# A bidirectional scan kernel: the stores of the raw diagonal blocks change their place and, in part, their queue

## What is computed

```
def step(S, inp):
    r_t, w_t, k_t, v_t, kk_t, kka_t = inp
    sa = einsum('bdhvk,bdhk->bdhv', S, kk_t)
    S = (S * w_t[..., None, :] - sa[..., :, None] * kka_t[..., None, :]
         + v_t[..., :, None] * k_t[..., None, :])
    return S, einsum('bdhvk,bdhk->bdhv', S, r_t)
```

## Time and profile before

| | us |
|---|---|
| three timed executions | 4001.73, 4027.17, 4028.21 (median 4027.17) |
| profiled execution, its own time | 3987.78 |
| its span in the trace | 3986.0 |
| TensorE busy | 3632.5 (91 %) |
| GpSimd busy | 1079.8 (27 %) |
| VectorE busy | 1378.7 (35 %) |
| ScalarE busy | 783.3 (20 %) |

### The profile page before, as it was taken

How to read it: one execution, slowest core, us unless ns; L and a number is a source line. 1 busy time by engine, 2 the same in 40 slices (tenths; PEclk the granted TensorE clock), 3 DMA queues, 4 the chain that set the end, 5 groups by cost and what they waited for, 6 DMA issues and landing times. The chain is left out here.

```text
span 3986.0 us, 64120 instructions
## 1 busy us (share of the span) xinstructions
PE 3632.5 (91%) x24967; PEld 2877.3 (72%) x24968; DVE 1378.7 (35%) x2811; ACT 783.3 (20%) x1467; POOL 1079.8 (27%) x1573
## 2 busy tenths in 40 slices
PE   8999999995799999999799999999999949999960
PEld 4777666663699889999788989989989934444420
DVE  2444444442345454454122222222222242222237
ACT  1222222222233333232111111111111101111113
POOL 0333333333555555555011011011011000000013
PEclk9999999997899999999899999999999969999985
DMA  8323222223323333332711011111011144765235
GB/s 290 106 100 105 97 95 91 91 96 136 88 74 97 102 101 101 95 91 52 244 69 64 35 41 64 35 41 64 35 41 64 41 166 164 258 230 185 89 111 206
DMA packets 297255, 424.33 MB, mean 106 GB/s; under 512 B 122446, under 2 KB 206156, under 8 KB 297036
## 3 DMA queue, kind: packets, MB, share of 16 engines
q1 hardware_dynamic: 268812, 309.84, 23.8%
q10 hardware_dynamic: 16272, 67.64, 4.5%
q0 software_dynamic: 11952, 43.52, 3.3%
HBM read 287.99 MB, written 132.94 MB: 106 GB/s over the span
## 5 line engine op out<-in xcount | busy, mean ns | idle before, releaser
L1757 PE MATMUL c_ps<-c_hT,big 128*128 128x128 f32 x6528 | 751.3, 276 | 27.3 <-DMA big<-in_w_in 27.3
L1757 PEld LDWEIGHTS c_ps<-c_hT,big 128*128 128x128 f32 x6528 | 742.6, 193 | 35.3 <-issue 30.1
L661 PE MATMUL a_ps<-a_win,a_hT 128*128 128x512 f32 (+1 forms) x1088 | 416.1, 540 | 3.8 <-DVE a_mix L572 3.8
L2180 PE MATMUL e_ps<-big,e_xT 128*128 x784 | 347.6, 597 | 2.3 <-DVE e_xT L2142 2.3
L661 PEld LDWEIGHTS a_ps<-a_win,a_hT 128*128 128x128 f32 x1088 | 204.0, 190 | 199.8 <-issue 187.0
L655 PE MATMUL a_ps<-a_hT,a_win 128*128 128x128 f32 x2992 | 343.9, 277 | 2.3 <-ACT a_hT L343 2.3
L655 PEld LDWEIGHTS a_ps<-a_hT,a_win 128*128 128x128 f32 x2992 | 340.6, 193 | 6.2 <-issue 2.9
L1110 POOL TENSOR_TENSOR b_tmp<-b_tt,b_ta 128x126 f32<-128x126 f32 (+22 forms) x527 | 203.7, 386 | 332.4 <-DMA b_ta<-s_a 269.5
L2180 PEld LDWEIGHTS e_ps<-big,e_xT 128*128 128x128 f32 x784 | 149.4, 191 | 191.8 <-issue 191.8
L1757 PE MATMUL c_ps<-c_wo,c_mT 128*128 128x512 f32 x544 | 236.3, 592 | 0.0
L1722 DVE TENSOR_TENSOR c_gs<-c_gs,c_ps 128x384 f32<-128x384 f32 x136 | 75.3, 554 | 445.1 <-PE c_ps L1757 434.9
(11 more groups left out here) (328 smaller groups left out, 5338.3 us busy)
## 6 DMA issues: line engine op xcount, KB each, us to landing
big<-in_exp_w SPq DMA_DIRECT2D x48, 1024.0 KB, 10.3
s_D<-a_shared SPq DMA_DIRECT2D x34, 768.0 KB, 5.9
s_yr<-e_yo ACTq DMA_DIRECT2D x49, 512.0 KB, 3.1
b_f<-s_D ACTq DMA_DIRECT2D x32, 768.0 KB, 7.9
a_aw<-in_ada_w SPq DMA_DIRECT2D x32, 512.0 KB, 6.6
b_f<-s_A ACTq DMA_DIRECT2D x32, 512.0 KB, 5.7
s_A<-a_shared SPq DMA_DIRECT2D x17, 768.0 KB, 3.4
big<-in_w_in SPq DMA_DIRECT2D x12, 1024.0 KB, 12.3
```

What stands on the lines that cost most here:

```text
L661: ins = nc.tensor.matmul(ps[:, bank, 0:width], hT[b][:, k, :], win[:, k, c:c + width], start=k == 0, stop=k == KD - 1)
L1757: return nc.tensor.matmul(out, lhsT, rhs, start=start, stop=stop)
L2180: return nc.tensor.matmul(out, lhsT, rhs, start=start, stop=stop)
```

## The change

diagonal_out is cut in three. The forward stores (from Ar) stay on SyncE, but stand in forward_out, which is called between the store of this tile's inverse and the loads of TZ; it waits for the copies of the forward Ar only. The backward stores (from AT) go to ScalarE's queue, in backward_out: after the copies of Ar, ahead of the start value of TT and of the loads of F. It waits for both halves of AT and until TA of the tile before has landed, since it overwrites what that load reads. diagonal_in, the loads of TA, stands where diagonal_out stood and waits for all eight stores. inverse_in is cut into inverse_out (the store) and inverse_in (the loads of TZ). No transfer is added, dropped or resized.

```diff
+        def diagonal_out(e, d, tile):
+            for i in range(4):
+                own = slice(SB * i, SB * i + SB)
+                at = 32 * d + 8 * i
+                e.dma_start(scr["a32"][at:at + 8].rearrange("s (r c) -> r s c", r=SB), tile[own, :, own]).then_inc(a_st, 16)
...
-                def diagonal_out(t, b):
+                def forward_out(t, b):
                     sp.wait_ge(const_in, 48)
                     after(sp, ar_ok[0][0], t)
                     after(sp, ar_ok[0][1], t)
-                    after(sp, at_ok, t, 2)
-                    for d, tile in ((0, Ar[0][b]), (1, AT)):
-                        for i in range(4):
...
+                    diagonal_out(sp, 0, Ar[0][b])
+
+                def diagonal_in(t):
                     sp.wait_ge(const_in, 48)
                     after(sp, a_st, t, 128)
...
-                diagonal_out(0, 0)
+                forward_out(0, 0)
+                diagonal_in(0)
...
+                    inverse_out(q)
+                    if left > 0:
+                        forward_out(q + 1, 1 - b)
                     inverse_in(q)
                     if left > 0:
-                        diagonal_out(q + 1, 1 - b)
+                        diagonal_in(q + 1)
...
+                def backward_out(t):
+                    after(act, at_ok, t, 2)
+                    if not (isinstance(t, int) and t == 0):
+                        after(act, ta_in, t - 1, 32)
+                    diagonal_out(act, 1, AT)
...
                 raw(0, 0)
+                backward_out(0)
                 act.wait_ge(clear_ok, 6)
...
                         raw(q + 1, 1 - b)
+                        backward_out(q + 1)
                         identity(q + 1)
```

More of the change, by code:

```diff
@@ L890, in diagonal_out, with inverse_out @@
                         sp.dma_start(flat(TA[64 * half:64 * half + 64, :, :]), scr["a32"]).then_inc(ta_in, 16)
-                def inverse_in(t):
+                def inverse_out(t):
                     sp.wait_ge(const_in, 48)
@@ L898, in inverse_in @@
                         sp.dma_start(rows, TT[64 * half:64 * half + 64, :, :]).then_inc(tt_st, 16)
+                def inverse_in(t):
                     sp.wait_ge(const_in, 48)
```

## The result

The changed kernel takes 4048.13 us (median of 20 runs, 4035.30 to 4059.32), the kernel before 3992.66 us (20 runs, 3977.89 to 4028.21). The ratio is 1.0131, with the 95% interval 1.0113 to 1.0148: **1.3% slower**, some 55 us, where 6.5 us less were forecast. That is above the forecast's range of 3978 to 4044. The baseline was off too: of the 17 further runs of the kernel before, 16 lie under the 4014.5 that the sum was applied to. With the median of 3992.66 the sum would have given 3986.

A forecast was written before the change was run, and what follows sets the result against it. TensorE was taken to set the pace, seldom waiting for the inverse; -4.2 us at the start and -2.3 us in tiles 5 and 7 gave -6.5 us, from a middle of 4014.5 to 4008 us, range 3978 to 4044.

The forecast's parts named there:

- (a): SyncE's queue in each tile: Ar's stores ahead of TZ take 1.82 us; TZ issued from 1406.9 instead of 1405.9.
- (b): ScalarE's queue: AT's four store issues, 1.94 us, are hidden by its 7.17 us idle before the copy into Xs.
- (c): F's loads start about 1410.5, not 1406.15, after nearly all of TZ is issued; tiles 5 and 7 save 2.3 us.
- The first rival: TZ's loads are caught beside F: up to 4.5 us in 15 tiles, up to 68 us; time 4042, chance 0.16.
- (d): Loads of F, tile 7: there by about 1419, wanted at 1423.71; costed at 0, bound 1 us per tile.
- (e): TA comes 3 to 5 us earlier in each tile, worth nothing, since GpSimd's inverse loop has air.
- (f): Start: TA goes 6.1 us earlier, loses 1.9 us beside F; gain 4.2 us, bounds 0.8 and 6.1.
- The second rival: Only issue time is saved: 1.9 us at the start, tiles 5 and 7 still wait; 4012 to 4013, chance 0.14.
- The clock: TensorE's six slow stretches, 23.0 us, all go (3985) or double (4031); chance 0.12 of shifting by four or more.
- (4): Sign in the changed profile: F landed before ScalarE wants it, no new idle time ahead of the exponentials.
- (5): Sign: GpSimd's wait before the inverse not gone but split, shorter before TA, longer elsewhere, without effect.
- (3): Sign: TensorE's stretch from Xs to AL5 takes 5.4 us wherever the clock is 1.00, tiles 5 and 7 too.

The follow-up runs named there:

- forward stores alone: Against the changed kernel, AT's stores go back to SyncE behind the TZ loads, Ar's stay ahead of them; 3996.43 us.
- before, F waits for TZ: Against the kernel before, ScalarE issues the loads of F only when all eight TZ loads of the tile have landed; 3988.11 us.

## Why the prediction was wrong

**(a) Forward stores: right in kind, short by 1 us.** Ar's stores take 2.82 us in tile 7, not 1.82; in tiles 2 to 13, which run in a loop, they take 2.5 to 3.4 us, since one of the four issues takes 1.1 to 2.0 us in place of 0.45 (1.46 in tile 7). The 1.82 was tile 0's row, from code that is written out, and it was no row of a time without F: F's first load is issued at 988.99, beside it. TZ itself is at the quick end, 3.77 us. So its issues end 6.9 us after the last copy of Ar, where 5.7 to 6.5 were reckoned.

**(b) Backward stores: right.** They start 3.4 us after that copy and take 1.89 us, hidden by ScalarE's idle time; the copy into Xs still waits for TensorE.

**(c) is the step that failed, with (a)'s missing 1 us in it.** F starts 5.6 us after the copy, as predicted (5.5). But the step says that F then comes "after nearly all of TZ is issued" and gives all of TZ 1.9 us to land. Its own numbers had TZ's issue ending at 5.7 to 6.5 us, so its last issue starting 0.45 us before that, from 0.25 us ahead of F's first to 0.55 behind it. "Nearly all" was the mistake: VectorE waits for the last load, and a wait is as long as the last load, not as the median. Five of eight landed about as said; the last took 9.1 us in tile 7, and 7.8 to 12.2 in the thirteen tiles.

The missing 1 us decided on which side the tiles fell. Tile 14 of the changed kernel is as the step had it: Ar's stores take 1.81 us, TZ's last issue starts level with F's first, the slowest load lands in 4.3 us, VectorE waits 0.46 us and TensorE not at all. In tile 1 Ar's stores take 1.81 us too, but one issue of TZ is slow, so that the eight take 4.51; the last one is 0.77 us behind F's first, and VectorE waits 4.70 us.

The first rival had the mechanism, and its sum of up to 68 us holds the measured 55: up to 4.5 us a tile, against 54.6 / 13 = 4.2. That its time of 4042 is so near 4048 is luck: it was added to a baseline 22 us too high, and took half of the waits. Its threshold was wrong: it was to decide from 1 us behind F's first issue, and it was given 0.16. The runs put it lower: level, 5.0 us to land; 0.6 us behind, 8.6 us (the longest landings in tiles 4 and 7 of the kernel with F 0.3 us later). The evidence against it, that "nothing should stretch Ar's issues", was wrong by the 1 us above.

That each DMA engine takes turns between queues, which the prediction cited from the Trainium skill ("DMA: Bandwidth & Descriptors", "Queues, rings and completion order"), agrees with the packets of this case. In the changed kernel's tile 7, from 1448.5 to 1451.0 us, while F moves in q10 and the rest of TZ in q1, SyncE's queue, the DMA view has (packets, MB, share of the 16 engines' time):

```profile
q10 hardware_dynamic: 207, 0.83, 91.6%
q1 hardware_dynamic: 228, 0.06, 12.3%
```

About one packet of the small load goes with each packet of F, which is some 4 KB (0.83 MB / 207), against 128 bytes in a row of TZ. The price, 9.1 us against 2.0 alone, is this case's.

**(d) F late: right at 0.** F lands by about 1445.05 + 11.7 = 1456.8 in tile 7, 18.9 us after the copy: the bound of the prediction, and 5 us later than its 14. No wait for it stands among the changed kernel's waits in tiles 1 to 13.

**(e) TA earlier: right that it is worth nothing, but not for the reason given.** In tile 7 it is issued 7.1 us after the copy instead of 13.8, but it lands 18.9 us after it, beside F, where before it landed after 19.3. So GpSimd had nothing to gain, and its air was not put to the test. Its row of the costliest groups names 294.0 us of waiting for TA, where before had 269.5:

```profile
L1129 POOL TENSOR_TENSOR b_tmp<-b_tt,b_ta 128x126 f32<-128x126 f32 (+22 forms) x527 | 203.9, 387 | 355.8 <-DMA b_ta<-s_a 294.0
```

**(f) The start: wrong in the size of sharing.** TA is issued 6.5 us earlier (6.1 predicted), but beside F it lands in up to 9.9 us instead of 4.1: it loses 5.8 us, where an equal turn was to cost 1.9. The first inverse starts 0.7 us earlier, about the lower bound of 0.8 rather than the 4.2 taken. And the first turn of TZ came 1.4 us later, not 4.2 earlier, because that inverse took 29.0 us instead of 27.1.

The second rival, that only issue time is saved, had this part right. With F held back, the time from Ar's first store to the first inverse is 997.47 - 989.12 = 8.4 us with AT's stores on ScalarE and 997.98 - 988.02 = 10.0 us with all stores on SyncE. So the second queue is worth 1.6 us, and holding F back some 5. The Trainium skill ("DMA: Bandwidth & Descriptors", "Issuing engines are not separate DMA queues") says that issuing on several engines at once saves only the time of the issue. This pair of runs agrees: four issues take 1.9 us.

**The clock** had little part in it: 30.5 us of slow stretches after, 25.2 before. Of the signs that the prediction named, (1) held, (4) held but for the start, where ScalarE's idle time ahead of the first exponentials grew from 7.0 to 10.1 us, (5) held only in that GpSimd's wait stayed (it was not split, and the part for TA grew), (2) failed in its first half (TZ 3.1 us after the copy, not 1.9), (6) failed, and (3) held for its stretch: the loss sat one stretch further, where I had set no sign, because I thought of TZ as one thing that VectorE waits for.

## To carry to other kernels

A small transfer that an engine waits for and a large one that it doesn't must be compared issue by issue, at the last piece of the small one: 1.4 us more delay of the large one was worth the whole 55 us here. The order costs only what the slack before the need does not cover, so a move that eats slack wakes a collision that was there before. Two edits that each cost nothing can meet, so a move is costed with the other's new times in place, not with the old ones. Holding the large transfer until the small one is issued is nearly free wherever the large one has slack: with F 1.4 us later ScalarE waited 61.3 us for F in all, instead of 24.0, and TensorE's waits for TZ were gone.

## What the runs showed that I had not expected

- A TZ load issued 0.9 us behind F's first took 11.5 us to land, level with it 5.0, and 0.4 us or more ahead of it (in the kernel with F 1.4 us later) at most 2.2: the price rises steeply within one microsecond, with the scatter told above.
- TensorE's wait for TZ is followed by products at half clock. In tile 7 the engine idled 4.03 us, then eight products took 2.05 us instead of 1.06 to 1.11 (granted clock of the stretch 0.68). The stretches to AL5, slow in five of the thirteen tiles before, were then all at full clock, so slow time hardly grew in total. Why is open.
- The 1 us that (a) lacked goes with a packet of the instruction queue. In each of tiles 1 to 13 of the changed kernel one issue of SyncE's takes 1.1 to 2.0 us (in tile 1 it is one of TZ's, in tiles 2 to 13 one of Ar's), and in each a packet of that queue starts 0.02 to 0.27 us ahead of it; in tile 7 the packet starts at 1438.07 and the slow issue at 1438.28. In tile 14 there is no slow issue. That the one causes the other was not tested.
- The first inverse takes 29.0 us, against 27.1 before. It is 27.1 that is rare: in all kernels the inverses of tiles 1 to 15 take 28.7 to 30.1 us. The 27.1 stands in the last tile of each, and in tile 0 of the kernel before and of two others (forward stores alone; before, F waits for TZ). It is 29.2 as well in the kernel before with F of tile 1 behind TA, where no store is moved, so the moved stores are not the reason. What is stays open.
